# GpSimd splits the weights of a large transformer kernel by chunks of 512 columns instead of by pairs of chunks

## The reference

```python
proj = h @ w_in                      # 1024 x 2072, then compressed, selected and windowed attention
x = x + rmsnorm(mix @ w_o)
gu = h @ w_gate_up                   # 1024 x 5632, then a short convolution, gelu and a gate
x = x + rmsnorm((gelu(a) * u) @ w_down)      # 2816 x 1024
x = x + (p @ w_ple) * sigmoid(x @ w_ple_gate)
# second block: two mixers, each modulated by vectors from c and c_ctx
m = silu(cvec) @ ada_w + ada_b       # 1024 x 3072, twice
y = diff_attention(h @ a_w_in, ...) @ w_out[0]     # 768 rows with the context, 8 heads
y = grouped_attention(h @ b_w_in, ...) @ w_out[1]
```

## Time and profile before

| | |
|---|---|
| runs | 1720.48, 1724.33, 1726.47 us, median 1724.33 us |
| profiled execution | 1720.3 us, its span 1719.0 us |
| granted TensorE clock, mean | 0.962 |
| PE busy | 1582.7 us (92% of the span) |
| DVE busy | 1124.3 us (65%) |
| POOL busy | 624.2 us (36%), 344 instructions |
| ACT busy | 622.1 us (36%) |

### The profile page before, as it was taken

The page is one execution under the profiler, slowest core; times in us unless marked ns, Lnnn a source line. Parts: engine busy times, 40 slices in busy tenths (PEclk is TensorE's granted clock), DMA queues, the critical chain, the costliest instruction groups (busy, mean ns, idle before and its releaser), DMA issues. The chain is left out here.

```text
span 1719.0 us, 21622 instructions
## 1 busy us (share of the span) xinstructions
PE 1582.7 (92%) x7933; PEld 1307.5 (76%) x7933; DVE 1124.3 (65%) x2136; ACT 622.1 (36%) x1506; POOL 624.2 (36%) x344
## 2 busy tenths in 40 slices
PE   5998899989999999999889999999997988899997
PEld 4876444777877788777688988898885777889886
DVE  7946666457777768888656666756676367665644
ACT  3213666231212220114443543454344356344331
POOL 5834000345655548475223113302333213323330
PEclk8987999999999999999999999999998999899999
DMA  6622000324434436563211011101111321111221
GB/s 182 205 60 86 1 1 1 135 85 137 124 115 127 121 95 231 159 204 113 92 50 50 10 41 50 49 2 49 50 39 60 134 75 50 50 50 38 62 86 49
DMA packets 115881, 142.55 MB, mean 83 GB/s; under 512 B 11048, under 2 KB 75200, under 8 KB 115776
## 3 DMA queue, kind: packets, MB, share of 16 engines
q1 hardware_dynamic: 89968, 91.77, 17.6%
q10 hardware_dynamic: 25808, 49.40, 8.6%
HBM read 132.74 MB, written 8.40 MB: 82 GB/s over the span
## 5 line engine op out<-in xcount | busy, mean ns | idle before, releaser
L468 POOL TENSOR_SCALAR w_hi<-w_raw 128x1024 fp32r<-128x1024 f32 x158 | 190.8, 1207 | 816.0 <-PE ps L482 623.6
L470 POOL TENSOR_TENSOR w_lo<-w_raw,w_hi 128x1024 fp32r<-128x1024 f32 x158 | 398.5, 2522 | 13.2
L480 PE MATMUL ps<-w_hi,h_hi 128*128 128x384 f32 (+2 forms) x768 | 283.0, 369 | 4.7 <-issue 2.6
L481 PE MATMUL ps<-w_lo,h_hi 128*128 128x384 f32 (+2 forms) x768 | 269.2, 351 | 0.0
L482 PE MATMUL ps<-w_hi,h_lo 128*128 128x384 f32 (+2 forms) x768 | 268.4, 349 | 0.0
L480 PE MATMUL ps<-h_hi,w_hi 128*128 128x512 f32 (+1 forms) x616 | 249.1, 404 | 5.1 <-DVE h_lo L2308 2.6
L481 PE MATMUL ps<-h_lo,w_hi 128*128 128x512 f32 (+1 forms) x616 | 241.4, 392 | 0.0
L482 PE MATMUL ps<-h_hi,w_lo 128*128 128x512 f32 (+1 forms) x616 | 240.8, 391 | 0.0
L2528 DVE SCALAR_TENSOR_TENSOR mod_acc<-mod_piece,csil,mod_acc 128x512 f32<-128x512 f32 x140 | 190.4, 1400 | 24.1 <-DMA mod_piece<-in_ada_w 19.0
L480 PEld LDWEIGHTS ps<-w_hi,h_hi 128*128 128x128 f32 x768 | 148.5, 193 | 16.7 <-issue 3.9
L482 PEld LDWEIGHTS ps<-w_hi,h_lo 128*128 128x128 f32 x768 | 148.0, 193 | 10.4
(11 more groups left out here) (322 smaller groups left out, 2846.5 us busy)
## 6 DMA issues: line engine op xcount, KB each, us to landing
mod_piece<-in_ada_w ACTq DMA_DIRECT2D x96, 256.0 KB, 3.1
w_raw<-in_w_gate_up SPq DMA_DIRECT2D x88, 256.0 KB, 3.1
w_raw<-in_a_w_in SPq DMA_DIRECT2D x128, 128.0 KB, 2.3
w_raw<-in_w_down SPq DMA_DIRECT2D x22, 512.0 KB, 4.0
w_raw<-in_b_w_in SPq DMA_DIRECT2D x20, 512.0 KB, 3.7
w_raw<-in_w_out SPq DMA_DIRECT2D x16, 512.0 KB, 3.8
w_raw<-in_w_in SPq DMA_DIRECT2D x8, 512.0 KB, 3.8
w_raw<-in_w_o SPq DMA_DIRECT2D x8, 512.0 KB, 3.7
```

Of the source, the lines that this page charges most:

```text
L468: pool.tensor_scalar(hi, raw, 1.0, 0.0, ALU.mult, ALU.add).then_inc(*s["pool_step"].up())
L470: pool.tensor_tensor(lo, raw, hi, ALU.subtract).then_inc(*s["w_split"].up(pair))
L480: pe.matmul(out, a[0], b[0], start=start, stop=False)
L481: pe.matmul(out, a[0], b[1], start=False, stop=False)
```

## The change

A pair is split in four instructions instead of two: the high half of the first chunk, its low half, then the high and the low half of the second chunk. `w_split` is raised once, by the last of them, so every wait of PE and SP stands where it stood. The wait of POOL on its own step now stands twice in a pair.

```diff
-            pool.tensor_scalar(hi, raw, 1.0, 0.0, ALU.mult, ALU.add).then_inc(*s["pool_step"].up())
-            pool.wait_ge(*s["pool_step"].now())
-            pool.tensor_tensor(lo, raw, hi, ALU.subtract).then_inc(*s["w_split"].up(pair))
+
+            for e in range(2):
+                pool.tensor_scalar(hi[:, e, :], raw[:, e, :], 1.0, 0.0, ALU.mult, ALU.add).then_inc(*s["pool_step"].up())
+                pool.wait_ge(*s["pool_step"].now())
+                m = pool.tensor_tensor(lo[:, e, :], raw[:, e, :], hi[:, e, :], ALU.subtract)
+            m.then_inc(*s["w_split"].up(pair))
```

## The result

The changed kernel is faster: 1714.35 us median of 5 runs (1713.10 to 1719.49) against 1724.33 of before, ratio 0.9947 with a 95% interval from 0.9926 to 0.9968. I had forecast 1732, slower. The time still lies inside my range of 1714 to 1743, at its lower edge; the range was drawn around a loss, so that is luck. Its profiled execution took 1713.1 us, 7.2 less than that of before.

A forecast was written before the change was run, and what follows sets the result against it. PE, busy 92% of the span, was taken to bound the kernel. Start 0, gate and up 0, down +3.5, heads +3.0, chains +4.0, L2858 and its like -2.8 gave +7.7: 1724.3 + 7.7 = 1732.0 us, range 1714 to 1743.

The forecast's parts named there:

- The cost of a pair: POOL's split in four instructions: 0.5 us more a pair, 4.0 instead of 3.5 undisturbed, 83 us of POOL over 166 pairs.
- Gate and up: 0: Gate and up products: no change, since the shortest lead of a pair there is 8.4 us.
- Start: 0.: Start of the kernel: pair 8 makes PE 3.6 us later, the 3.44 us wait at 97.73 goes; 0 in sum.
- Down: +3.5: Down stage: late pairs 75 and 79 cost 5.8 us, ACT's waits give back 2.9, pairs 84 to 86 add 0.6.
- Heads: +3: Six attention heads: POOL's longer burst holds DVE instructions, 0.5 us slower a head, 3.0 us in all.
- Square-root chains: +4.: Three chains of tiny DVE instructions beside POOL's splits (1374, 1442, 1477) end later: +1.5, +1.2 and +1.3 us.
- DVE's instruction L2858: Two large DVE instructions at 1307.05, taking 4.47 us beside POOL's halves, would end 1.8 us earlier.
- The place before the first head: A spot ahead of the first head where large DVE instructions in a row meet POOL: 1.0 us gained.
- Rival A: POOL's blocks of DVE on the chain of waits halve and PE gets it all: -17 us, 1707; chance 0.22.

The follow-up runs named there:

- e2_not_ff: Against the kernel before: all pairs except the gate and up ones split a chunk at a time; 1726.76 us, ratio 1.0029.
- e10_heads: Against the kernel before: only the pairs of the heads split a chunk at a time; 1728.57 us, ratio 1.0030.
- e5_ff_lo: Against the kernel before: only in gate and up pairs, low half made in two instructions, high half whole; 1714.85 us, ratio 0.9952.
- e1_ff: Against the kernel before: only the gate and up pairs split a chunk at a time; 1709.51 us, ratio 0.9915.
- e7_table2: Against the kernel before: POOL's split untouched, DVE's gate and up accumulations spread evenly, two in each slot; 1720.44 us, ratio 0.9984.
- e4: Against the kernel before: POOL's split untouched, DVE's gate and up accumulations moved between slots, (2, 3) and (3, 1); 1739.36 us, ratio 1.0090.
- e9: Against the kernel before: POOL's split untouched, six discarded PE products ahead of each gate and up sum; 1733.24 us, ratio 1.0067.

## Why the prediction was wrong

**The cost of a pair** was right: 0.62 and 1.29 us for undisturbed halves against 0.63 and 1.3, POOL 708.9 us against 700 or more, 0.5 us a pair. DVE's accumulations fell from a mean of 1.40 to 1.17 us, where I had said about 1.2.

**Gate and up: 0** is the step that failed, by 13.7 us of the 14.9 by which the sum missed the profiled executions (+7.7 forecast, -7.2 measured). The other errors, of both signs, nearly cancel. I asked only whether a pair comes late for PE, and its lead of 8.4 us answered that. But I had worked out, for the start, that DVE needs 1.4 instead of 2.1 us an instruction beside POOL. The same accumulations run in this stage, and PE waits for them at four sums. Those waits were in the list of the kernel before; "issue" as their releaser hid who was waited for. And the first of these waits, 1.03 us, stood for 4.4, since 6.8 us at half clock came behind it, which I never looked up.

**Start: 0.** PE waited for pairs 7 and 8, 1.87 and 2.22 us, at the places foretold, and the wait at 97.73 was gone. The sum was 2.1 better, since DVE's second stream was done before PE came.

```profile
54.45 0.50 PE L483 MATMUL ps<-h_hi,w_hi 128*128 128x512 f32 x1 [1.87 <-POOL w_lo L472]
58.33 0.50 PE L483 MATMUL ps<-h_hi,w_hi 128*128 128x512 f32 x1 [2.22 <-POOL w_lo L472]
94.75 4.07 PE L885 MATMUL ps<-small,mod_acc 128*128 128x1 f32 x32
```

**Down: +3.5**, measured 4.7. Pair 75 was 3.7 late, not 2.0, because PE came some 15 us earlier and POOL's splits only 12.9: pair 74 was begun at 641.49 instead of 654.36, after a wait of 2.66 us for its load. Pair 79 was in time, pair 90 late. ACT's waits at 703.92 and 712.47 went, as foretold. The total is near, its parts are not.

**Heads: +3**, measured 9.1. The mechanism was right to the instruction: POOL's longer burst meets the last rotation, PE's wait grows by 0.69 us a head, and all waits by 3.0. What was missing is the price of half clock behind the longer wait, some 6 us.

**Square-root chains: +4.** The one at 1442 has more and shorter holds, as foretold, but lasts 7.5 us against 7.4, not 1.5 more. DVE's instruction L2858 takes 2.98 us instead of 4.47, 1.5 of the 1.8 foretold. The stretch from 1288 to the end wins 1.8 us, where I had a loss of 2.2 (4.0 less 1.8). The place before the first head, to which I gave 1.0, lies in a stretch (769 to 903) that wins 3.7; which wait gave the rest wasn't followed up.

**Rival A**, the blocks halve, was right in its sign (1707), but by another way. The heads, of which it expected 8 us, lost 9, and its gain came in a stage that it didn't name. For the rule of the Trainium skill that it rested on ("SBUF — State Buffer", "Who interferes with whom"), the traces agree: a DVE instruction that meets POOL gets through behind that one instruction: the rotation at 985.70 takes 1.37 us, 0.42 undisturbed, and ends 0.3 us behind the half of 1.38 at 985.41. What decides is how many it meets on the way to a wait of PE.

## What to carry to other kernels

For each wait of the engine that bounds the kernel, ask who is waited for, also where the view says "issue", and whether the change reaches that engine; the lead of the thing that is changed is only one of the ways. Price a wait of TensorE together with the clock behind it. Where GpSimd and VectorE share a stream, cut GpSimd's instructions where VectorE is waited for, and leave them long where GpSimd's burst itself must end early: that choice by stage is worth some 11 to 13 us here over the same cut everywhere.

## What the hardware did that I had not expected

A short wait of TensorE can cost more through the clock than by its length. Ahead of the sums of the gate and up stage, waits of 1.0 to 1.5 us came with 3.4 to 6.8 us at the clock's lower level in the kernel before, but with none in four other cases (1.25 us in e2_not_ff, 1.18 in e10_heads, 1.40 in e5_ff_lo, 1.19 in e1_ff). Waits of 2.3 us came with 3.4 (e7_table2), and all eight of 3.9 to 6.2 us with 10.2 (e2, e4, e9, e10). In the heads of the kernel before, 1.60 us came with none or 3.4; in those of the changed kernel, 2.28 to 2.66 us with 3.4 to 6.8, six times of six. The sum's small products alone, with a wait below 0.2 us or none, were followed by 3.4 us several times (the window from 424.70 above), so that a wait's length alone doesn't say what comes behind it.

VectorE and GpSimd, both busy on SBUF, take turns instruction by instruction: 2.1, 1.3 and 0.94 us for a VectorE instruction that alone takes 0.75, with GpSimd's pair in two, four and eight.
